# Attention scores masked by VectorE in PSUM, with ScalarE copying the products with V and turned v

## The chip, the cores and the metric

The kernel runs on one core of a Trainium2 chip. A core has four engines that matter here, each with its own list of instructions, in order: TensorE (matrix products and the turning of tiles, which write PSUM), VectorE, ScalarE and GpSimd; SyncE issues the loads. Semaphores order them. The metric is the device time of one execution in microseconds (us), the median of several runs.

## The reference, cut to what matters

Two blocks follow each other. The first one is two layers of attention on 1024 tokens behind 16 meta tokens (L = 1040), in float32. Each layer has 4 "diff" heads, each with two score maps whose softmaxes are subtracted, and 8 "fox" heads with a forget term. Scores are masked: in diff heads by chunks of 64 tokens, in fox heads causally.

```python
# diff: chunk_ids is 0 for the meta tokens, then one number for each 64 tokens
s = einsum('bhmqd,bhmkd->bhmqk', qb, k) * scale
s = where(chunk_ids[None, :] <= cq[:, None], s, -inf)
p = softmax(s)
a = p[:, :, 0] - lam * p[:, :, 1]
o = einsum('bhqk,bhkd->bhqd', a, v)
# fox
s = einsum('bhqd,bhkd->bhqk', qb, k) * scale + cq[..., None] - cum_logf
s = where(positions[None, :] <= pq[:, None], s, -inf)
o = einsum('bhqk,bhkd->bhqd', softmax(s), v)
```

The second block (retention, a Fourier mix, a convolving feed-forward part) isn't touched by the change.

## The kernel before, in words

Products are made from split numbers: each float32 operand is kept as a high part rounded for TensorE (WH, AH, QH, KH) and a low rest (WL, AL, QL, KL), and three products (high by high, high by low, low by high) stand for one. ScalarE rounds the weights (L1596), VectorE makes the rests (L2173).

A layer's attention has 8 groups g of 128 rows: g below 4 is one diff head with its two maps m, g of 4 and more ("fox" in the code) two fox heads. Its work is a list of steps:

- a unit (`step_unit`, L1048) is one eighth of a projection's chunk of 344, 352 or 512 columns: three products with all 128 rows of the array. Projections of later groups fill the time between the other steps;
- scores (`step_scores`, L1094): for a block j of 128 query rows (j = 0 to 7; 8 is the 16 meta rows, in layer 0 alone) the scores of both maps. Their width W is 16 + 128 (j + 1), or 16 for j = 8. Map m uses rows 64m to 64m + 63 of the array, so products of the two maps stand in pairs. Each span of PSUM up to a bank's edge (512 columns) has three products, in fox a fourth with the forget term (C2, selr). Then come the mask products (`masks`, L1118): eyer, an identity of 64 rows, by maskr, which adds -1e30 at the hidden places. Diff has one on the last 64 columns, none at j = 8; fox one on the last 128 (16 at j = 8) and one on the last 64, cut at the banks' edges. Scores have one region of PSUM for each map (`region`, L351), so a block's scores wait for the exp of the block before;
- max (`step_max`, L2350): VectorE reduces each map's row maximum from PSUM; exp (`step_exp`, L1732): ScalarE makes exp(s - max) into P and its row sum; norm (`step_norm`, L2360): VectorE scales P;
- tr (L1152): TensorE turns tiles of P into one of the banks 5, 6 and 7 (`turn_bank`, L1041); pt: ScalarE (L1755) or VectorE (L2392 to L2395) copies them out;
- turn_v (L1085) turns v into such a bank, v_out (`step_v_out`, L2337) copies it to V, four tiles of 128 x 128 at a time and one of 16 x 128;
- av (L1170) makes the products of turned P with V in such a bank, av_out (`step_av_out`, L2397) copies them to OTt, which is gated (L2429), stored by GpSimd and loaded again at the layer's end. A group's first av_out waits for the store of the group before.

The order of the steps is written by a planner, `attention_order` (L761), with a class `Clocks` (L399): it keeps a time for each engine, gives each step a cost (`cost`, L439, for TensorE; `side_of`, L575, for the others), and places the step that can begin next, by rank. Each engine then takes its own steps from that one list. `PRIORITY` and `ACT_STEPS` (L402 to L405) say how side steps rank and which of them are ScalarE's. The wait of a copy stands in front of it on whichever engine it is.

At the start, ScalarE's `step_set_up` (L1674) copies the constants eyer, maskr and selr from where SyncE's loads put them, inside V (L158, L3115), and the first v_out waits for that. Of the lines in the trace, L977 is every matrix product and L986 every turning.

Of the kernel before, what the change touches and what calls it, by code (L numbers as in the profile page):

```python
# [7 lines left out]
F32R = mybir.dt.float32r  # L8
ALU = mybir.AluOpType
# [94 lines left out]
def build(nc, A, S, O):  # L104

    ctx = ExitStack()
    with ctx:
# [50 lines left out]
        SELF, MASKF = Vf[:, 0:1024], Vf[:, 1024:1664]  # L158
# [240 lines left out]
        class Clocks:  # L399
# [5 lines left out]
            ACT_STEPS = ("leave", "exp", "rope_end", "split", "fin1", "root", "reload")  # L405
# [33 lines left out]
            def cost(self, st):  # L439
# [135 lines left out]
            def side_of(self, st):  # L575
# [462 lines left out]
        def tensor_attention(e, l):  # L1038
# [55 lines left out]
            def step_scores(g, j):  # L1094
                fox = g >= 4
                if l == 0 and g == 0:
                    e.wait_ge(*const_split.at(0))
# [20 lines left out]
                def masks(m, a, b):  # L1118

                    r = slice(64 * m, 64 * m + 64)  # L1120
                    d0 = 0 if j == 8 else W - 128
                    if fox:
                        c0, c1 = max(a, d0), b
                        if c0 < c1:
                            yield eyer[r, 0, :], maskr[r, 1, c0 - d0:c1 - d0], c0, c1
                    if j != 8:
                        c0, c1 = max(a, W - 64), b
                        if c0 < c1:
                            yield eyer[r, 1 if fox else 0, :], maskr[r, 2 if fox else 0, c0 - W + 64:c1 - W + 64], c0, c1
# [452 lines left out]
        def scalar(e):  # L1582
# [79 lines left out]
            def attention(l):  # L1662
# [61 lines left out]
                def step_rope_end(g, kind, ci):  # L1724
# [5 lines left out]
                    e.activation((QH if kind == "q" else KH)[:, g % 2, c:c + n], TMP[:, c:c + n], ACT.Copy).then_inc(*qk_hi.mark(key))  # L1730

# [54 lines left out]
                do = {"split": step_split, "leave": step_leave, "fill": step_fill, "stats": step_stats, "set_up": step_set_up, "forget": step_forget, "rope_end": step_rope_end, "exp": step_exp, "pt": step_pt,  # L1786
# [379 lines left out]
        def vector(e):  # L2166
# [74 lines left out]
            def attention(l):  # L2241
# [95 lines left out]
                def step_v_out(g, quad):  # L2337
                    vs = g % 2
                    b = banks.place.get(("vt", l, g, quad), 0)
                    e.wait_ge(*vt_mm.at((l, g, quad)))  # L2340
                    if quad == 0 and g == 0 and l == 0:
                        e.wait_ge(*const_split.at(0))
                    if quad == 0 and g >= 2:
                        e.wait_ge(*av_mm.at((l, g - 2, len(BLOCKS[l]) - 1)))
                    if quad < 2:
                        e.tensor_copy(V[:, vs, 4 * quad:4 * quad + 4, :], bank(b).rearrange("p (a b) -> p a b", a=4)).then_inc(*v_turned.mark((l, g, quad)))
                    else:
                        e.tensor_copy(V[0:NM, vs, 8, :], bank(b)[0:NM, 0:128]).then_inc(*v_turned.mark((l, g, quad)))
# [48 lines left out]
                def step_av_out(g, bi):  # L2397
                    blk = BLOCKS[l][bi]
                    meta = blk == (8,)
                    nq = NM if meta else 256  # L2400
                    q0 = 0 if meta else NM + 128 * blk[0]
                    b = banks.place.get(("av", l, g, bi), 0)
                    e.wait_ge(*av_mm.at((l, g, bi)))
                    if bi == 0:
                        if g:
                            e.wait_ge(*o_stored.at((l, g - 1)))
                        elif l:
                            e.wait_ge(*fill_tr.at((1, 4, 7)))
                    e.tensor_copy(OTt[:, q0:q0 + nq], bank(b)[:, 0:nq]).then_inc(*av_out.mark((l, g, bi)))

# [26 lines left out]
                def step_stats(p):  # L2437
# [3 lines left out]
                      "forget": step_forget, "rope_sin": step_rope_sin, "rope_add": step_rope_add, "rope_lo": step_rope_lo, "v_out": step_v_out,  # L2441
                      "max": step_max, "norm": step_norm, "pt": step_pt, "av_out": step_av_out, "fin_ms": step_fin_ms, "fin3": step_fin3,
# [657 lines left out]
        def sync(e):  # L3100
# [14 lines left out]
            e.dma_start(MASKF, A["k_mask"]).then_inc(*const_in[1].landed(0))  # L3115
# [54 lines left out]
def host_constants():  # L3170
# [4 lines left out]
    r = np.arange(64)  # L3175
    m = np.zeros((2, 64, 5, 128), f)
    for a in range(2):
        m[:, r, a, 64 * a + r] = 1.0
    m[:, :, 2, 0:64] = NEG
    m[:, :, 3] = np.where(q[None, :] <= r[:, None], 0.0, NEG)  # L3180
    m[:, :, 4, 0:64] = np.where(r[None, :] <= r[:, None], 0.0, NEG)
    c["k_mask"] = m.reshape(128, 640)
# [100 lines left out]
```

## Time and profile before

| what | us |
|---|---|
| median of 3 runs | 2811.51 |
| the runs | 2808.3, 2811.51, 7464.21 |
| the profiled execution | 2806.45 |
| its span, first to last instruction | 2804.6 |
| the attention of layer 0, about | 80 to 743 of the span |
| the attention of layer 1, about | 890 to 1510 of the span |

All durations below come from the profiled execution. Busy time of TensorE counts overlapping products once, and the row of one product lasts longer than the distance to the next one's start, since products are pipelined; the distance between starts tells what one costs. The granted clock is 2.4 GHz nearly throughout (a mean of 0.99 of it).

### The profile page before, as it was taken

The page shows a single profiled execution, that of the slowest core. Times are in us where ns is not written, and L with a number is a line of the kernel's source. Part 1 is how long each engine was busy: PE and PEld are TensorE (multiplying, and loading weights), DVE is VectorE, ACT ScalarE, POOL GpSimd, SP SyncE. Part 2 cuts the span into 40 slices and gives each one's busy share as a digit, 9 for nine tenths or more (in the row PEclk, how much of TensorE's full clock was granted, in tenths as well). Part 3 has the DMA queues.
Part 4 walks back from the last instruction along what each step waited for, and adds up shares of the span by engine and source line. Part 5 has one row for each costly group of instructions (what it writes and reads, how often), then busy time and mean ns, then how long its engine had stood idle before and what let it go on. Part 6 is the DMA issues. An engine that isn't in the chain of part 4 may idle for free.

```text
span 2804.6 us, 42406 instructions
## 1 busy us (share of the span) xinstructions
PE 2731.3 (97%) x17076; PEld 2347.9 (84%) x17076; DVE 1533.5 (55%) x2769; ACT 1035.8 (37%) x1967; POOL 258.6 (9%) x392
## 2 busy tenths in 40 slices
PE   6999999999999999999999999999999999999999
PEld 6788888888899888877787988888998888888887
DVE  5766654555546666655445485564365444455335
ACT  5434333333334444433334562224362222223232
POOL 1211100000002122000002060000030000000000
PEclk9999999999999999999999999999999999999999
DMA  4111211111312212122114132212331111111113
GB/s 151 62 62 58 74 59 59 59 57 62 130 63 67 70 63 80 59 65 71 63 38 143 59 109 65 60 38 97 106 113 46 53 45 53 46 50 56 53 60 128
DMA packets 149185, 200.11 MB, mean 71 GB/s; under 512 B 8806, under 2 KB 117030, under 8 KB 148990
## 3 DMA queue, kind: packets, MB, share of 16 engines
q1 hardware_dynamic: 128064, 134.20, 15.3%
q0 software_dynamic: 20928, 63.20, 6.3%
q8 instruction: 137, 2.24, 0.3%
q14 instruction: 56, 0.46, 0.1%
HBM read 162.66 MB, written 32.58 MB: 70 GB/s over the span
## 4 chain that ended last, share of the span: by engine, by line
PE 85%; DVE 6%; ACT 3%; issue 3%; DMA 2%; POOL 1%; DVEq 0%; SPq 0%; ACTq 0%; POOLq 0%
PE PS L977 80%; PE PS L986 5%; DMA T<-TMP 2%; DVE ST L2358 1%; DVE AL L2216 1%; POOL TMP L2979 0%; DVE WL L2173 0%; ACT top L1742 0%; DVE TMP L2328 0%; POOL T L2976 0%; DMA s_os<-OTt 0%; DVE T L2321 0%; DVE top L2371 0%; ACT WH L1596 0%; ACT TMP L1718 0%
## 5 line engine op out<-in xcount | busy, mean ns | idle before, releaser
L977 PE MATMUL PS<-AH,WH 128*128 128x512 f32 (+3 forms) x2528 | 941.7, 372 | 18.7 <-DVE AL L2216 9.3
L977 PE MATMUL PS<-AL,WH 128*128 128x512 f32 (+3 forms) x2528 | 895.1, 354 | 0.0
L977 PE MATMUL PS<-AH,WL 128*128 128x512 f32 (+3 forms) x2528 | 894.4, 354 | 0.0
L977 PEld LDWEIGHTS PS<-AH,WH 128*128 128x128 f32 x2528 | 477.1, 189 | 91.8 <-issue 18.3
L977 PEld LDWEIGHTS PS<-AH,WL 128*128 128x128 f32 x2528 | 476.7, 189 | 48.0
L977 PEld LDWEIGHTS PS<-AL,WH 128*128 128x128 f32 x2528 | 478.1, 189 | 45.0 <-issue 1.0
L977 PE MATMUL PS<-WH,AH 128*128 128x256 f32 (+1 forms) x1016 | 326.4, 321 | 4.0 <-DVE WL L2173 3.1
L2173 DVE TENSOR_TENSOR WL<-W,WH 128x1024 fp32r<-128x1024 f32 x184 | 225.6, 1229 | 185.0 <-ACT WH L1596 185.0
L977 PE MATMUL PS<-WL,AH 128*128 128x256 f32 (+1 forms) x1016 | 325.6, 320 | 0.0
L977 PE MATMUL PS<-WH,AL 128*128 128x256 f32 (+1 forms) x1016 | 325.5, 320 | 0.0
L2358 DVE TENSOR_REDUCE ST<-PS 128x1 f32<-128x784 f32 (+8 forms) x272 | 187.6, 731 | 126.9 <-PE PS L977 126.8
L1596 ACT ACTIVATE WH<-W 128x1024 fp32r<-128x1024 f32 x184 | 193.4, 1053 | 160.7 <-PE PS L977 140.4
L1742 ACT ACTIVATE top<-PS,ST 128x784 f32<-128x784 f32 (+8 forms) x272 | 195.1, 723 | 142.3 <-DVE ST L2358 115.7
L977 PEld LDWEIGHTS PS<-WH,AH 128*128 128x128 f32 x1016 | 193.7, 191 | 20.6 <-DVE WL L2173 3.9
L977 PEld LDWEIGHTS PS<-WL,AH 128*128 128x128 f32 x1016 | 193.7, 191 | 13.9
L977 PEld LDWEIGHTS PS<-WH,AL 128*128 128x128 f32 x1016 | 193.7, 191 | 13.6
L986 PE MATMUL PS<-ident,top 128*128 128x128 f32 (+2 forms) x1132 | 172.6, 276 | 12.7 <-DVE AL L2216 3.0
L977 PE MATMUL PS<-top,V 128*64 128x256 f32 (+6 forms) x1176 | 182.5, 371 | 1.4 <-DVE top L2395 0.8
L2092 ACT ACTIVATE R<-PS,R 128x512 f32<-128x512 f32 x88 | 68.4, 779 | 295.4 <-PE PS L977 295.4
L977 PEld LDWEIGHTS PS<-top,V 128*64 128x64 f32 (+3 forms) x1176 | 119.2, 154 | 64.8 <-issue 36.9
L2893 DVE SCALAR_TENSOR_TENSOR R<-PS,R 128x504 f32<-128x504 f32 x88 | 65.3, 742 | 185.7 <-ACT R L2092 185.7
L986 PEld LDWEIGHTS PS<-ident,top 128*128 128x128 f32 (+2 forms) x1132 | 125.5, 132 | 45.2 <-ACT top L1755 6.9
(341 smaller groups left out, 3347.8 us busy)
## 6 DMA issues: line engine op xcount, KB each, us to landing
W<-in_k_w_in SPq DMA_DIRECT2D x66, 512.0 KB, 3.9
W<-in_w_ada SPq DMA_DIRECT2D x48, 512.0 KB, 4.9
W<-in_w_up SPq DMA_DIRECT2D x44, 512.0 KB, 3.8
W<-in_w_in SPq DMA_DIRECT2D x28, 512.0 KB, 3.7
W<-in_w_out SPq DMA_DIRECT2D x24, 512.0 KB, 3.4
W<-in_w_down SPq DMA_DIRECT2D x22, 512.0 KB, 3.6
R<-s_xs POOLq DMA_DIRECT2D x16, 512.0 KB, 6.9
s_adap<-AST POOLq DMA_DIRECT2D x48, 128.0 KB, 4.4
```

The source lines that it names most:

```text
L977: return e.matmul(out, lhsT, rhs, start=start, stop=stop, skip_group_check=True)
L986: return e.transpose(out, in_, ident[0:k, 0:k])
L1596: e.activation(high(v), W32[:, s, :], ACT.Copy).then_inc(*w_hi.mark(v))
L1742: e.activation(P[0:rows, P_SLOT[u], 0:W], PSf[0:rows, o:o + W], ACT.Exp, bias=st[:, 0:1], accum_out=st[:, 1:2]).then_inc(*exped.mark(u))
L2092: e.activation(dst[:, c:c + n], bank(b), ACT.Identity, scale=CW[:, 1, jj:jj + 1], bias=CW[:, 3, jj:jj + 1]).then_inc(*conv_a.mark((j, ab, ...
L2173: e.tensor_tensor(low(v), W32[:, slot32(v), :], f(high(v)), ALU.subtract).then_inc(*w_lo.mark(v))
L2216: e.scalar_tensor_tensor(lo, bank(b)[:, o:o + n], COLS[:, 8 * l + k:8 * l + k + 1], f(hi), ALU.mult, ALU.subtract).then_inc(*fill_lo.mark( ...
L2358: e.tensor_reduce(ST[0:rows, ST_SLOT[u], 0:1], PSf[0:rows, o:o + W], AX.X, ALU.max, negate=True).then_inc(*row_max.mark(u))
L2893: e.scalar_tensor_tensor(d3[:, :, 1:64], o3[:, :, 0:63], CW[:, 0, jj:jj + 1], d3[:, :, 1:64], ALU.mult, ALU.add).then_inc(*conv_v.mark((j, ...
```

## The change

TensorE's mask products go, and with them eyer and maskr. A tile MK of its own takes the mask constants as they are loaded: a causal 128 x 128 one for both maps side by side, and a 64 x 64 one of -1e30 for the upper half of a diff block's rows. VectorE's `step_max` adds the mask to both maps in PSUM with one instruction (its pattern spans both regions), marks a semaphore, waits for it, and then makes the two reductions. Diff blocks add on 64 rows and 2 x 64 columns, fox blocks on 128 rows and 2 x 128 columns (16 rows and 2 x 16 at j = 8), diff j = 8 nothing. av_out and v_out are ScalarE's, with the same waits. The planner's costs follow.

```diff
-            eyer = own("eyer", [128, 2, 128], F32R)
-            maskr = own("maskr", [128, 3, 128], F32R)
+            MK = own("MK", [128, 640])[:, :]
...
+        CAUSAL, BLOCKED = MK[:, 0:256].rearrange("p (m n) -> p m n", m=2), MK[0:64, 256:384].rearrange("p (m n) -> p m n", m=2)
...
-            ACT_STEPS = ("leave", "exp", "rope_end", "split", "fin1", "root", "reload")
+            ACT_STEPS = ("leave", "av_out", "v_out", "exp", "rope_end", "split", "fin1", "root", "reload")
...
-                    return sum((4 if g >= 4 else 3) * max(110, 8 + 0.44 * (b - a)) for a, b in cut) + (250 if j != 8 else 0) + (90 if g >= 4 else 0)
+                    return sum((4 if g >= 4 else 3) * max(110, 8 + 0.44 * (b - a)) for a, b in cut)
...
-                    return max(at[("scores",) + st[1:]], at[("normed",) + self.stats[i - 4]] if i >= 4 else 0.0), 300 + 2.08 * width(st[2])
+                    return (max(at[("scores",) + st[1:]], at[("normed",) + self.stats[i - 4]] if i >= 4 else 0.0),
+                            300 + 2.08 * width(st[2]) + (450 if st[1] >= 4 else 320 if st[2] != 8 else 0))
...
-                if l == 0 and g == 0:
+                if l == 0 and g == 4:
                     e.wait_ge(*const_split.at(0))
...
-                        row += [(q, k, c0, c1, False) for q, k, c0, c1 in masks(m, a, b)]
...
                 def step_set_up():
                     e.wait_ge(*const_in[1].at("all"))
-                    e.activation(eyer[:, :, :].rearrange("p a b -> p (a b)"), MASKF[:, 0:256], ACT.Copy)
-                    e.activation(maskr[:, :, :].rearrange("p a b -> p (a b)"), MASKF[:, 256:640], ACT.Copy)
...
+                    e.activation(OTt[:, q0:q0 + nq], bank(b)[:, 0:nq], ACT.Copy).then_inc(*av_out.mark((l, g, bi)))
...
+                        e.activation(V[:, vs, 4 * quad:4 * quad + 4, :], bank(b).rearrange("p (a b) -> p a b", a=4), ACT.Copy).then_inc(*v_turned.mark((l, g, quad)))
...
                 def step_max(g, j):
                     rows, W = (NM if j == 8 else 128), width(j)
+                    fox = g >= 4
+                    for m in range(2):
+                        e.wait_ge(*score_mm[m].at((l, g, j)))
+                    if fox or j != 8:
+                        if l == 0 and g == 0:
+                            e.wait_ge(*const_in[1].at("all"))
+                        n = min(W, 128) if fox else 64
+                        mask = CAUSAL[0:rows, :, 0:n] if fox else BLOCKED
+                        a, apart = region(j, 0) + W - n, region(j, 1) - region(j, 0)
+                        late = PSf[0:rows if fox else 64, a:a + 2 * apart].rearrange("p (m n) -> p m n", m=2)[:, :, 0:n]
+                        e.tensor_tensor(late, late, mask, ALU.add).then_inc(*row_max.mark((l, g, j, "masked")))
+                        e.wait_ge(*row_max.at((l, g, j, "masked")))
                     for m in range(2):
...
-                        e.wait_ge(*score_mm[m].at((l, g, j)))
...
-                    e.tensor_copy(OTt[:, q0:q0 + nq], bank(b)[:, 0:nq]).then_inc(*av_out.mark((l, g, bi)))
...
-            e.dma_start(MASKF, A["k_mask"]).then_inc(*const_in[1].landed(0))
+            e.dma_start(MK, A["k_mask"]).then_inc(*const_in[1].landed(0))
```

## Rows read from the trace of the kernel before

**Rows 1.** The page: busy time, share of the span and instructions of each engine.

```profile
PE 2731.3 (97%) x17076; PEld 2347.9 (84%) x17076; DVE 1533.5 (55%) x2769; ACT 1035.8 (37%) x1967; POOL 258.6 (9%) x392
```

**Rows 2.** Busy time by stretch: us, PE, PEld, DVE, ACT, POOL, clock, DMA share, GB/s.

```profile
80.00:743.00 663.00, 643.07 (x4683) 554.05 (x4681) 392.68 (x867) 253.99 (x543) 64.11 (x101) 0.99 0.19 64
890.00:1510.00 620.00, 606.30 (x4167) 497.49 (x4164) 371.80 (x777) 247.00 (x494) 62.07 (x94) 1.00 0.20 66
...
1490.00:1510.00 20.00, 16.47 (x135) 11.37 (x135) 17.91 (x45) 12.77 (x27) 1.58 (x3) 0.98 0.25 79
```

**Rows 3.** Waits of TensorE in 80 to 743 us: us, times, longest.

```profile
PE PS L977 <- DVE OTt L2409: 3.1, 4, 2.5
...
PE PS L977 <- ACT top L1742: 1.3, 3, 0.5
```

**Rows 4.** Waits of TensorE in 890 to 1510 us.

```profile
PE PS L977 <- ACT top L1742: 5.5, 10, 1.3
```

**Rows 5.** The tile maskr: its products, min/median/max ns, first and last start, forms.

```profile
L977 PE MATMUL PS<-maskr,eyer x416: 182/234/267, 88.8 to 1503.3; 64*128 64x64 f32 x77, 64*128 64x128 f32 x40, 64*128 64x16 f32 x13, 64*128 64x48 f32 x8
```

**Rows 6.** Timeline of TensorE around a fox step, 912 columns: start, us, engine, instruction.

```profile
503.99 0.31 PE L977 MATMUL PS<-AH,WL 128*128 128x344 f32 x1
504.23 0.50 PE L977 MATMUL PS<-KH,QH 64*128 64x512 f32 x2
...
505.81 0.34 PE L977 MATMUL PS<-C,selr 64*128 64x400 f32 x2
505.99 0.30 PE L977 MATMUL PS<-maskr,eyer 64*128 64x128 f32 x4
506.23 0.42 PE L977 MATMUL PS<-AH,WH 128*128 128x344 f32 x1
```

**Rows 7.** The same around the end of a diff step, 528 columns.

```profile
125.93 0.28 PE L977 MATMUL PS<-KH,QL 64*128 64x256 f32 x2
126.05 0.19 PE L977 MATMUL PS<-maskr,eyer 64*128 64x64 f32 x2
126.17 0.43 PE L977 MATMUL PS<-AH,WH 128*128 128x344 f32 x1
```

**Rows 8.** The same around the end of a diff step of 16 columns, without mask.

```profile
159.02 0.26 PE L977 MATMUL PS<-KL,QH 64*128 64x16 f32 x2
...
159.13 0.26 PE L977 MATMUL PS<-KH,QL 64*128 64x16 f32 x2
...
159.32 0.43 PE L977 MATMUL PS<-AH,WH 128*128 128x344 f32 x1
```

**Rows 9.** Groups of VectorE by shape: count, busy us, mean ns, idle before.

```profile
L2409 DVE COPY OTt<-PS 128x256 f32<-128x256 f32 x64 | 27.1, 423 | 83.7 <-PE PS L977 77.4 <-DMA s_os<-OTt 6.4
...
L2346 DVE COPY V<-PS 128x512 f32<-128x512 f32 x32 | 20.7, 684 | 7.7 <-PE PS L986 7.7
...
L2308 DVE SCALAR_TENSOR_TENSOR GT<-GT,PS 128x344 f32<-128x344 f32 x16 | 8.1, 509 | 15.1 <-ACT GT L1711 15.0
```

**Rows 10.** Groups of ScalarE by shape.

```profile
L1755 ACT ACTIVATE top<-PS 128x512 f32<-128x512 f32 x101 | 59.4, 597 | 82.1 <-PE PS L986 81.4
...
L1755 ACT ACTIVATE top<-PS 16x256 f32<-16x256 f32 x61 | 22.6, 372 | 115.5 <-PE PS L986 115.5
```

**Rows 11.** Timeline of ScalarE's set-up copies.

```profile
50.34 0.41 ACT L1676 ACTIVATE eyer<-V 128x256 fp32r<-128x256 f32 x1
...
50.65 0.51 ACT L1677 ACTIVATE maskr<-V 128x384 fp32r<-128x384 f32 x1
```

**Rows 12.** Timeline of the first block of layer 0, with idle time and its releaser.

```profile
92.22 1.13 ACT L1742 ACTIVATE top<-PS,ST 128x1040 f32<-128x1040 f32 x1 [2.29 <-DVE ST L2358]
...
92.84 0.38 PE L986 MATMUL PS<-ident,TMP 128*16 128x128 f32 x1 [2.44 <-DVE V L2346]
```

**Rows 13.** Timeline: two VectorE instructions, the second of which reads the first's result.

```profile
94.91 0.75 DVE L2371 TENSOR_SCALAR top<-top,ST 128x1040 f32<-128x1040 f32 x1
...
95.78 1.30 DVE L2374 SCALAR_TENSOR_TENSOR top<-top,ST 128x1040 f32<-128x1040 f32 x1
```

More of the change, by code:

```diff
@@ L157, in build @@
         Vf = V.rearrange("p s t n -> p (s t n)")
-        SELF, MASKF = Vf[:, 0:1024], Vf[:, 1024:1664]
+        SELF = Vf[:, 0:1024]
+        CAUSAL, BLOCKED = MK[:, 0:256].rearrange("p (m n) -> p m n", m=2), MK[0:64, 256:384].rearrange("p (m n) -> p m n", m=2)
         LAMT, LAMP = GT[:, 0:512].rearrange("p (l a n) -> p l a n", l=2, a=4), GT[:, 512:640].rearrange("p (a n) -> p a n", a=2)
@@ L1116, in terms @@
                         yield selr[r, 2 * (g - 4) + m, :], C2[r, a:b]
[L1118 to L1129, printed above, removed]
                 cuts = [[(x - region(j, m), y - region(j, m)) for x, y in pieces(region(j, m), region(j, m) + W)] for m in range(2)]
@@ L1730, in step_rope_end, with step_av_out, step_v_out @@
                     e.activation((QH if kind == "q" else KH)[:, g % 2, c:c + n], TMP[:, c:c + n], ACT.Copy).then_inc(*qk_hi.mark(key))
+                def step_av_out(g, bi):
+                    blk = BLOCKS[l][bi]
+                    meta = blk == (8,)
+                    nq = NM if meta else 256
+                    q0 = 0 if meta else NM + 128 * blk[0]
+                    b = banks.place.get(("av", l, g, bi), 0)
+                    e.wait_ge(*av_mm.at((l, g, bi)))
+                    if bi == 0:
+                        if g:
+                            e.wait_ge(*o_stored.at((l, g - 1)))
+                        elif l:
+                            e.wait_ge(*fill_tr.at((1, 4, 7)))
+                    e.activation(OTt[:, q0:q0 + nq], bank(b)[:, 0:nq], ACT.Copy).then_inc(*av_out.mark((l, g, bi)))
+                def step_v_out(g, quad):
+                    vs = g % 2
+                    b = banks.place.get(("vt", l, g, quad), 0)
+                    e.wait_ge(*vt_mm.at((l, g, quad)))
+                    if quad == 0 and g == 0 and l == 0:
+                        e.wait_ge(*const_split.at(0))
+                    if quad == 0 and g >= 2:
+                        e.wait_ge(*av_mm.at((l, g - 2, len(BLOCKS[l]) - 1)))
+                    if quad < 2:
+                        e.activation(V[:, vs, 4 * quad:4 * quad + 4, :], bank(b).rearrange("p (a b) -> p a b", a=4), ACT.Copy).then_inc(*v_turned.mark((l, g, quad)))
+                    else:
+                        e.activation(V[0:NM, vs, 8, :], bank(b)[0:NM, 0:128], ACT.Copy).then_inc(*v_turned.mark((l, g, quad)))
                 def step_exp(g, j):
@@ L1784, in step_stats @@
                     norm_stats(l, p)
-                do = {"split": step_split, "leave": step_leave, "fill": step_fill, "stats": step_stats, "set_up": step_set_up, "forget": step_forget, "rope_end": step_rope_end, "exp": step_exp, "pt": step_pt,
+                do = {"split": step_split, "leave": step_leave, "fill": step_fill, "stats": step_stats, "set_up": step_set_up, "forget": step_forget, "rope_end": step_rope_end, "exp": step_exp, "av_out": step_av_out, "v_out": step_v_out, "pt": step_pt,
                       "fin1": step_fin1, "root": step_root, "reload": step_reload}
@@ L2335, in step_rope_lo @@
                     e.tensor_tensor(lo[:, g % 2, c:c + n], TMP[:, c:c + n], f(hi[:, g % 2, c:c + n]), ALU.subtract).then_inc(*qk_lo.mark(key))
[L2337 to L2348, printed above, removed]
                 def step_max(g, j):
                     rows, W = (NM if j == 8 else 128), width(j)
+                    fox = g >= 4
[10 more added lines that the diff above has]
+                        e.wait_ge(*row_max.at((l, g, j, "masked")))
                     for m in range(2):
@@ L2395, in step_pt @@
                         e.tensor_copy(PT[:, pt, part[1], 128:256], bank(b)[:, 384:512]).then_inc(*pt_dve.mark(key))
[L2397 to L2408, printed above, removed]
-                    e.tensor_copy(OTt[:, q0:q0 + nq], bank(b)[:, 0:nq]).then_inc(*av_out.mark((l, g, bi)))
                 def step_fin_ms(g, ci):
@@ L2440, in attention @@
                 do = {"split_lo": step_split_lo, "leave_lo": step_leave_lo, "fill": step_fill, "stats": step_stats, "set_up": step_set_up, "ada_out": step_ada_out,
-                      "forget": step_forget, "rope_sin": step_rope_sin, "rope_add": step_rope_add, "rope_lo": step_rope_lo, "v_out": step_v_out,
-                      "max": step_max, "norm": step_norm, "pt": step_pt, "av_out": step_av_out, "fin_ms": step_fin_ms, "fin3": step_fin3,
+                      "forget": step_forget, "rope_sin": step_rope_sin, "rope_add": step_rope_add, "rope_lo": step_rope_lo,
+                      "max": step_max, "norm": step_norm, "pt": step_pt, "fin_ms": step_fin_ms, "fin3": step_fin3,
                       "gate": step_gate, "reload_lo": step_reload_lo}
@@ L3174, in host_constants @@
     q = np.arange(128)
[L3175 to L3182, printed above, removed]
+    m = np.zeros((128, 640), f)
+    m[:, 0:256] = np.tile(np.where(q[None, :] <= q[:, None], 0.0, NEG), 2)
+    m[0:64, 256:384] = NEG
+    c["k_mask"] = m
     s = np.zeros((128, 8, 128), f)
```

## The prediction, made before the change was run

> **What bounds the kernel now.** The page comes first: TensorE is busy 97% of the span, VectorE 55%, ScalarE 37% [rows 1]. The change touches only the two attention stretches, so the table by stretch is next: in 80 to 743 us TensorE is busy for 643.1 of 663 us, in 890 to 1510 for 606.3 of 620 [rows 2]. It therefore stands still for 19.9 + 13.7 = 33.6 us there. VectorE has 392.7 + 371.8 = 764.5 us of work in these 1283 us (60%), ScalarE 254.0 + 247.0 = 501 us (39%). Then the waits of TensorE by releaser: for the exp that frees the score banks 1.3 us in 3 waits and 5.5 us in 10, for VectorE's copy of a product with V 3.1 us [rows 3, 4]. Attention is bound by TensorE's own work, and time taken out of that work is gained as long as what replaces it stays beside it. Other parts of the kernel are left alone.
>
> **Part 1, the mask products leave TensorE.** There are 416 [rows 5]. By the code: a diff step with j of 0 to 6 has two (one pair, the halves m = 1 and 0 run side by side on 64 rows each), j = 7 has three; a fox step has four, j = 7 six, j = 8 two. Over both layers 68 x 2 + 136 x 2 + 8 = 416 (block 8 is in layer 0 alone).
> What one costs is read between starts, since durations overlap. In a fox step the four begin at 505.99 and the next projection unit at 506.23: 0.24 us [rows 6]. In a diff step 126.05 to 126.17: 0.12 us [rows 7]. If all of that went, the sum would be 56 x 0.12 + 56 x 0.25 + the sixteen j = 7 steps at about 0.25 and 0.6 + four j = 8 steps at 0.2: 6.7 + 14 + 2 + 4.8 + 0.9 = 28 us, and some 33 us if the mixed ends of the steps (masks ahead of a transposition or a product with V, not shown) are up to a sixth dearer. This is the upper bound.
> But part of this interval isn't the mask's. In the other direction, from a unit of 344 columns (503.99) to the first score pair (504.23), 0.24 us pass [rows 6]; 344 columns at 2.4 GHz are 0.143 us, so changing between 128-row and 64-row products costs about 0.1 us. The diff pair of 64 columns is 0.027 us of streaming; 0.12 less 0.027 leaves the same 0.09. That gap stays when the mask goes: it then stands behind the last score pair. So a diff mask gives back only its streaming, 0.03 us. The next limit is the weight load: pairs of 16 columns follow each other every 0.11 us [rows 8]. Where the last score pair is short (144 columns, j = 0 and 4), the mask pair waited for its load, and 0.05 us more goes. In a fox step the second pair (64 columns) is loaded while the first streams, so it costs a whole load: 0.11 + 0.03 = 0.14 us. Step by step: diff 40 x 0.03 + 16 x 0.08 = 2.5; diff j = 7, 8 x 0.2 = 1.6 (two short loads in one half); fox 40 x 0.14 + 16 x 0.19 = 8.6; fox j = 7, 8 x 0.37 = 3.0 (three to four loads in one half); j = 8, 4 x 0.11 = 0.4. Sum 16 us. This is the lower bound, and the one I take, because the two gaps of rows 6 and 7 agree on it.
> The Trainium skill says the same of the gap, in "TensorEngine Tiling (Array Packing)", section "Key Properties": changing the tiling mode drains TensorE. By that rule the gap is owed at every change, mask or no mask, and the sum is 16 us; without it it would be 28 to 33. The trace agrees as far as it goes (0.24 us behind a unit, 0.12 behind a mask pair), but has no wide score step without a mask to show it.
>
> **Part 2, VectorE's masks.** 64 fox steps get an addition on 128 x 256 elements of PSUM, 64 diff steps one of 64 x 128, four one of 16 x 32: 132 in all. No row shows an addition that writes PSUM. The nearest reads it: 128x344 in 509 ns, and 128x512 copied in 684 ns, so 151 ns and 1.04 ns an element [rows 9]. That gives 0.42 us and 0.28 us. Below, the 0.12 us of hand-over could be hidden; above, I allow 0.1 us for the write into PSUM. The first reduction reads the result and waits for it; between two such dependent instructions 95.66 to 95.78 pass, 0.12 us [rows 13]. Added: 64 x 0.42 + 64 x 0.28 + 0.7 + 132 x 0.12 = 61 us.
> The wait for the scores isn't new: the reductions waited for the same products. What is behind it in VectorE's queue (its copies of turned P, the low halves of the weights) gets each time 0.4 to 0.54 us later, and so does the exp, which frees the single pair of score regions.
>
> **Part 3, the copies go to ScalarE.** VectorE loses 64 copies at 423 ns and 32 at 684 ns [rows 9], with 16 of 128 columns (0.28 us by the same rule) and 8 of 16: 27 + 21 + 4.5 + 1.3 = 54 us. So VectorE ends at +7 us, 60% busy as before. ScalarE takes them at 372 ns for 256 columns and 597 ns for 512 [rows 10]: 24 + 19 + 4 + 1.4 = 48 us, 549 of 1283 us, 43% busy. Neither becomes the bound by its work. But a copy on ScalarE now stands behind two exps (1.13 us each for the widest block [rows 12]), and the copy frees one of TensorE's three turning banks. TensorE waited 3.1 us for these copies in the first stretch [rows 3]; I let it lose 2 us more. VectorE's 6.4 us of waiting for the store of the last group's output [rows 9] goes to ScalarE with the copy; the exps behind it are then held, 0 to 6 us, taken as 0, since the list of steps is planned with the store's due time.
> One place gains. At 92.84 TensorE has waited 2.44 us for VectorE's copy of turned v, which stood behind two reductions, while ScalarE was idle for 2.29 us before its exp at 92.22 [rows 12]. There the copy gets done at once: 0 to 2.4 us, I take 2.
>
> **Part 4, set-up and loads.** ScalarE's two copies into eyer and maskr go: 0.41 + 0.51 us [rows 11]. They stand ahead of the rounding of the weights for which TensorE waits at about 58 us, so 0.9 us is gained, 0 at worst. SP issues the same two loads; the mask's lands in a tile of its own.
>
> **Part 5, the order.** The planner gets new costs (TensorE's 250 and 90 ns go, 450 and 320 come to VectorE, the copies to ScalarE), so the interleaving changes throughout. It can't win more than what TensorE now stands still, 33.6 us, and a poorer fit could cost as much as a third of that again. The latency has a plainer price: TensorE waited 13 times for the exp that frees the score banks; each grows by about 0.4 us, together +5 us. The end of layer 1 is the tight place: in 1490 to 1510 VectorE is busy 17.9 of 20 us [rows 2]; four steps' masks (2 us) enter and three copies (1.3 us) leave, +0.7 us, part of these 5.
>
> **Sum.** -16 - 0.9 - 2 + 5 + 2 = -12 us. The profiled execution took 2806.45 us (span 2804.6): 2794.5 us. The fast two of the runs shown are 2808.3 and 2811.5, 2 to 5 us above it, so I say 2795 us. A measurement of this kernel can tell about 2% (56 us) from no change.
>
> **Rivals.**
> - The whole interval of the masks goes (28 to 33 us), the array's change being hidden under the wide score pair. For: the next weights could load meanwhile. Against: rows 6. 2806.5 - 30 - 2.9 + 7 = 2780 us, 2777 with 33.
> - Given back: ScalarE's queue order and the changed plan cost what TensorE gains, some 12 us more than counted. For: TensorE's waits in attention are only 33.6 us because the plan fits so well. 2806 us.
> - Slower: the turn-round of the score banks. The banks are held from the first score product to the second exp; the mask lengthens this by 0.54 less 0.14 us in fox, 0.40 less 0.03 in diff, about 0.4 us a step. Once the steps at which TensorE runs out of other work pass 19 / 0.4 = 48 of 136, the gain is gone; the trace has 13. At 90 steps it is +36 - 19 = +17 us: 2824 us; at all 136 (no product's time gained, the chain alone deciding) +54, 2860 us. Against it: the same 13 waits, 6.8 us in 1283, so the chain has slack at the other 123 steps.
>
> **How the numbers follow.** Forecast 0.50, whole interval 0.17, given back 0.18, turn-round 0.15. The forecast's own range is 2786 to 2803. The range goes from the whole interval with its larger sum (2777, less 2) to halfway between given back and turn-round: 2775 to 2813. Over 2% faster (below 2750) needs more than all mask intervals and both gains, 36 us: 0.02. Over 2% slower needs every step in the chain and more: 0.02. Within 2%: 0.96.
>
> **What would show it.** TensorE without any maskr rows and 416 instructions fewer, busy time and start-to-start of the stretches down by some 16 us; a fox step of 8 pairs (912 columns) taking 1.86 us where it was 2.00 [rows 6], and a gap of about 0.1 us behind its last pair beyond streaming. If it takes 1.75, the first rival holds. An addition row of about 420 and 285 ns, and the reduction 0.12 us behind it. Waits of TensorE for the exp up from 6.8 us to about 12; if they are above 25 us, the turn-round holds. ScalarE 48 us busier. I am wrong if attention gets longer, or if TensorE's waits move by more than 15 us in either direction.

## The result, and the profile after

The changed kernel takes 2817.14 us (median of 12 runs, 2811.24 to 2819.25) against 2810.8 us for the kernel before on the same chip: a ratio of 1.0023, 95% interval 1.0015 to 1.0031. That is within the 2% called "same", but it is a small loss where a gain of 12 us was forecast, and it lies above the range. The profiled execution has a span of 2816.8 us (2804.6 before).

The page's busy line of the kernel after:

```profile
PE 2727.8 (97%) x16660; PEld 2335.5 (83%) x16660; DVE 1536.0 (55%) x2778; ACT 1078.1 (38%) x2088; POOL 261.3 (9%) x392
```

TensorE has exactly 416 instructions fewer [rows 1], ScalarE 42 us more work, VectorE as much as before. By stretch (columns as in [rows 2]):

```profile
80.00:743.00 663.00, 638.17 (x4464) 546.20 (x4464) 398.29 (x872) 274.32 (x606) 66.47 (x101) 0.98 0.20 66
890.00:1510.00 620.00, 598.53 (x3904) 485.36 (x3900) 360.58 (x756) 260.55 (x533) 60.67 (x92) 0.98 0.20 63
```

TensorE stands still for 24.8 + 21.5 = 46.3 us where it was 33.6, and the clock is 0.98 in both stretches where it was 0.99 and 1.00. The new instructions, by shape (the first two to be held against the forecast of 420 and 280 ns, the last two against 372 and 597):

```profile
L2361 DVE TENSOR_TENSOR PS<-PS,MK 128x256 f32<-128x256 f32 x64 | 27.6, 431 | 93.3 <-PE PS L978 93.0
L2361 DVE TENSOR_TENSOR PS<-PS,MK 64x128 f32<-64x128 f32 x64 | 18.4, 288 | 49.2 <-PE PS L978 48.9
...
L1729 ACT ACTIVATE OTt<-PS 128x256 f32<-128x256 f32 x64 | 24.6, 384 | 133.9 <-PE PS L978 129.8 <-DMA s_os<-OTt 4.1
L1740 ACT ACTIVATE V<-PS 128x512 f32<-128x512 f32 x32 | 17.3, 594 | 18.7 <-PE PS L987 18.7
```

The fox step of 912 columns, which went from 504.23 to 506.23 [rows 6], in TensorE's timeline after:

```profile
508.72 0.50 PE L978 MATMUL PS<-KH,QH 64*128 64x512 f32 x2
...
510.29 0.36 PE L978 MATMUL PS<-C,selr 64*128 64x400 f32 x2
510.58 0.43 PE L978 MATMUL PS<-AH,WH 128*128 128x344 f32 x1
```

510.58 - 508.72 = 1.86 us, as forecast, not 1.75. The last pair streams 400 columns (0.17 us at 2.4 GHz) and the next unit starts 0.29 us behind it: 0.12 us are owed for the change of products, mask or not. The first rival ends here.

Now the waits. TensorE's in 80 to 743 us, then in 890 to 1510 us:

```profile
PE PS L978 <- ACT top L1754: 8.0, 6, 2.8
PE PS L978 <- DVE top L2402: 3.7, 2, 2.0
PE PS L987 <- ACT TMP L1703: 3.2, 1, 3.2
```

```profile
PE PS L978 <- ACT top L1754: 9.9, 7, 3.4
PE PS L978 <- DVE FIN L2411: 4.8, 3, 2.9
```

Those for the exp (L1754, L1742 before [rows 3, 4]) are again 13, but 17.9 us in place of 6.8, with single ones of 2.8 and 3.4 us where the longest was 1.3. An addition of 0.43 us can't make such a wait. The longest, with all engines, in order of time (idle time and releaser in brackets):

```profile
1088.95 1.23 DVE L2425 SCALAR_TENSOR_TENSOR OTt<-OTt,GT 128x1024 f32<-128x1024 f32 x1
...
1090.09 0.22 DVE L2377 RECIPROCAL ST<-ST 128x1 f32<-128x1 f32 x2
...
1090.58 0.60 POOL L2979 DMA_DIRECT2D s_os<-OTt  x1 [7.26 <-DVE OTt L2425]
...
1091.13 0.90 DVE L2384 SCALAR_TENSOR_TENSOR top<-top,ST 128x656 f32<-128x656 f32 x1
1091.24 0.28 PE L978 MATMUL PS<-KH,QL 64*128 64x256 f32 x2
...
1091.95 0.42 DVE L2265 COPY AST<-PS 128x256 f32<-128x256 f32 x1
1092.29 0.28 DVE L2361 TENSOR_TENSOR PS<-PS,MK 64x128 f32<-64x128 f32 x1
1092.60 1.32 DVE L2368 TENSOR_REDUCE ST<-PS 128x1 f32<-128x528 f32 x2
1093.34 0.70 ACT L1754 ACTIVATE top<-PS,ST 128x528 f32<-128x528 f32 x1 [2.79 <-DVE ST L2368]
...
1094.62 0.20 ACT L1754 ACTIVATION_READ_ACCUMULATOR top<-PS,ST 128x1 f32 x1
1094.91 0.70 PE L978 MATMUL PS<-KH,QH 64*128 64x400 f32 x2 [3.39 <-ACT top L1754]
```

The scores of 528 columns end at 1091.5, and TensorE's next step is the scores of 400 columns, for which there is no room until both exps have read the scores. VectorE is behind: the gate of the group that ends here and the last block's normalisation are ahead of the addition, and only then come the two reductions and the exps. TensorE takes its list in order, so what stands behind the scores waits with them. The new order has four such places (202.35, 286.33, 1010.31 and 1094.91 us), score step directly behind score step; the old order has none. What follows a long wait is seen behind the second of them:

```profile
286.33 0.70 PE L978 MATMUL PS<-KH,QH 64*128 64x400 f32 x2 [2.74 <-ACT top L1754]
...
288.37 0.49 PE L978 MATMUL PS<-AH,WL 128*128 128x344 f32 x1
288.66 0.49 PE L978 MATMUL PS<-AH,WH 128*128 128x344 f32 x1
...
292.62 0.32 PE L978 MATMUL PS<-AH,WL 128*128 128x344 f32 x1
292.78 0.32 PE L978 MATMUL PS<-AH,WH 128*128 128x344 f32 x1
```

Up to about 292.5 the same products of 344 columns start every 0.29 us, afterwards every 0.16: 344 columns take 0.287 us at 1.2 GHz and 0.143 at 2.4. The trace's record of the granted clock has 6.8 us at the lower level here, from 285.71 to 292.54, so it fell 0.6 us before the wait ended. (The Trainium skill, "TensorE: Matmul & The Clock Gate", Part 1, says that an idle TensorE is put to half rate; the trace agrees.)

**An account of the attention.** Three numbers of a trace say where each kernel's time goes, from 85 us to the start of its last score step: the gaps between TensorE's products; the time in which products ran at 1.2 GHz by the record of the granted clock (half of which is lost; the part of a slow stretch that falls into a gap is in the gaps already and is left out); and the rest, which is work at 2.4 GHz. All in us. The first column is the median of the kernel's runs; the others are of one profiled execution each, which lies up to 6 us from that median (both_copies_order's took 2781.3). The kernels of the next section are in the table too:

| kernel | median | last score step | gaps | products at 1.2 GHz | last - gaps - half |
|---|---|---|---|---|---|
| before | 2810.8 | 1502.7 | 33.6 | 9.3 | 1464.4 |
| after | 2817.1 | 1514.1 | 49.4 | 44.2 | 1442.7 |
| masks_old_order | 2808.9 | 1504.9 | 44.8 | 19.6 | 1450.3 |
| both_old_order | 2822.2 | 1515.5 | 51.3 | 31.0 | 1448.7 |
| copies_old_order | 2825.9 | 1523.3 | 41.9 | 34.1 | 1464.3 |
| new_order_alone | 2855.5 | 1554.2 | 67.5 | 53.8 | 1459.8 |
| no_masks_old_order | 2800.6 | 1498.6 | 36.9 | 25.2 | 1449.1 |
| copies_own_order | 2788.3 | 1487.2 | 23.8 | 13.0 | 1456.9 |
| both_copies_order | 2786.7 | 1480.6 | 30.8 | 13.7 | 1443.0 |
| fox_masks_copies_order | 2784.0 | 1481.4 | 29.1 | 13.4 | 1445.6 |
| two_pairs | 2797.8 | 1499.3 | 40.5 | 31.7 | 1442.9 |
| one_pair | 2806.7 | 1505.9 | 44.2 | 34.1 | 1444.7 |
| no_pairs | 2814.7 | 1509.6 | 49.1 | 32.9 | 1444.1 |

After against before: 21.8 us less of work, 15.7 us more of gaps, 17.5 us more lost to the clock, +11.4 at the last score step. The work saved was real; more than all of it went to gaps and the clock. Not all of the 21.8 us is the mask products: the four pairs of kernels that share an order and differ in the masks differ by 14.0 to 17.2 us, and the rest goes with the order (new_order_alone, with every product of before, has 4.6 us less work than before).

### The profile page after: what moved, and what is told of

Its sections match the earlier page's. It is cut to its first block, busy times and chain, and to the rows that moved or that the text cites. A ratio compares the mean times of both kernels' runs of the same rounds, so it can differ in the third digit from the quotient of the medians.

```text
span 2816.8 us, 41701 instructions
## 1 busy us (share of the span) xinstructions
PE 2727.8 (97%) x16660; PEld 2335.5 (83%) x16660; DVE 1536.0 (55%) x2778; ACT 1078.1 (38%) x2088; POOL 261.3 (9%) x392
## 4 chain that ended last, share of the span: by engine, by line
PE 87%; DVE 4%; ACT 3%; issue 3%; DMA 2%; POOL 0%; SPq 0%; ACTq 0%; DVEq 0%; POOLq 0%
PE PS L978 82%; PE PS L987 5%; DMA T<-TMP 1%; DVE AL L2228 1%; ACT top L1754 0%; DVE WL L2185 0%; DVE ST L2368 0%; DMA s_os<-OTt 0%; ACT TMP L1595 0%; ACT TMP L1703 0%; ACT R L1888 0%; ACT L1780 0%; ACT R L1820 0%; ACT WH L1583 0%; POOL T L2972 0%
## 5 line engine op out<-in xcount | busy, mean ns | idle before, releaser
L1754 ACT ACTIVATE top<-PS,ST 128x784 f32<-128x784 f32 (+8 forms) x272 | 194.9, 722 | 121.9 <-DVE ST L2368 101.6
```

The costliest lines, as they stand in the source:

```text
L1754: e.activation(P[0:rows, P_SLOT[u], 0:W], PSf[0:rows, o:o + W], ACT.Exp, bias=st[:, 0:1], accum_out=st[:, 1:2]).then_inc(*exped.mark(u))
```

## The experiments

Two words recur. **Old order** means that the planner lists the steps as for the kernel before, whatever the engines then do. **Own order** means that it is given the costs of what is kept. Theories under test at first: the masks' latency ate the gain; the copies on ScalarE ate it; or the new order did. The letters in an expectation are explained in it. All ratios are to the kernel before on the same chip, with the 95% interval. The groups of kernels ran on different chips, on which the kernel before took 2808.5 to 2810.8 us, so a difference of two medians can be off by some 2 us; the difference of the two ratios is given beside it where that matters.

**1. The order, and each part in the old order.** Four kernels. both_old_order is the changed kernel with the planner's lines as before:

```
-            ACT_STEPS = ("leave", "av_out", "v_out", "exp", ...)
+            ACT_STEPS = ("leave", "exp", ...)
-                    return sum(...)
+                    return sum(...) + (250 if j != 8 else 0) + (90 if g >= 4 else 0)
-                            300 + 2.08 * width(st[2]) + (450 if st[1] >= 4 else 320 if st[2] != 8 else 0))
+                    ... 300 + 2.08 * width(st[2])
```

> Edit: the changed kernel with the planner's costs and its list of ScalarE steps as they were before, so every engine goes by the list of steps of the kernel before. Theory A (the new order is what lost the time: TensorE gives back 14 us of mask products as it should, and the list planned with the new costs puts score steps where they wait): 2795 to 2802 us, 9 to 16 us under before, TensorE's waits in attention no more than 8 us above before's, no new stretch at 1.2 GHz. Theory B (the mask in the chain from scores to exp costs this directly, wherever it is put): 2812 us or more, and TensorE's waits for the exp up by 10 us or more. Theory C (the copies behind the exps in ScalarE's queue): also above 2808 us, with waits of TensorE for the copies at their ScalarE lines.

masks_old_order also takes step_av_out and step_v_out back to VectorE (tensor_copy), copies_old_order instead takes the mask products back and the additions out, and new_order_alone is the kernel before with the three planner edits of the change alone.

> Edit: the masks on VectorE alone; the copies stay on VectorE, and the order is that of before. Theory A: 2797 to 2804 us, VectorE 61 us busier. Theory B: above 2812 us, as with the copies moved. Theory C: 2797 us or less, clearly under the run with the copies on ScalarE.

> Edit: the kernel before with the two kinds of copies on ScalarE alone; masks stay products, order of before. Theory A: 2805 to 2812 us, within 4 us of before. Theory B: the same. Theory C: 2815 us or more, with TensorE waiting for the copies more than 10 us.

> Edit: the kernel before in every instruction, but planned with the changed costs and with the copies counted as ScalarE's, so only the order of the steps is new. Theory A: 2822 to 2835 us, the 16 us of waits and some 27 us more at 1.2 GHz being all there (mask products stay, so 14 us more than the changed kernel at most). Theories B and C: 2806 to 2815 us, like before.

Measured: both_old_order 2822.2 us, 1.0047 [1.0034, 1.0059]; masks_old_order 2808.9 us, 0.9995 [0.9987, 1.0004]; copies_old_order 2825.9 us, 1.0063 [1.005, 1.0076]; new_order_alone 2855.5 us, 1.0164 [1.015, 1.0178]. So the masks are neutral, the copies lose 17 us in an order that was not made for them, and an order made for other engines costs 46 us with no work changed. Theory A's ranges missed all four: the old order did not bring the changed kernel back (2822 us for 2795 to 2802), and new_order_alone, slower as it said, came out 20 us above its range. masks_old_order fits none of the three theories. Theory C was right for copies_old_order. What that kernel loses is, by the account, 8.3 us of gaps and 12.4 us of clock. Among TensorE's waits in 80 to 743 us are:

```profile
PE PS L977 <- DVE GT L2335: 6.3, 3, 3.0
PE PS L977 <- ACT V L1755: 4.0, 4, 3.4
PE PS L986 <- ACT OTt L1744: 3.0, 2, 1.5
```

The last two are copies. That they wait their turn in a list of ScalarE's that was not made for them is my reading; the run of part 3 that changes the list alone bears it out.

**2. What the additions cost.** The changed kernel without them, in the old order with the copies on VectorE; the masks are left out, so this kernel computes attention unmasked:

```
-                        e.tensor_tensor(late, late, mask, ALU.add).then_inc(...)
-                        e.wait_ge(*row_max.at((l, g, j, "masked")))
```

> Edit: as masks_old_order, with VectorE's mask addition and its wait left out, so the scores aren't masked at all; order of before. What this leaves is TensorE's saving alone. If the saving is real and VectorE's mask in the chain gives it back (theory D: latency): 2793 to 2799 us, 10 to 16 us under masks_old_order. If time freed on TensorE is lost anyway, because the other engines' chains hold the places where it stalls (theory E: no cover): 2803 to 2809 us, with TensorE's idle time up by what was saved.

Measured 2800.6 us, 0.996 [0.9947, 0.9972]. The additions, 132 of them, cost 2808.9 - 2800.6 = 8.3 us (10 by the ratios) where the prediction had 5. The time lies between the ranges of D and E. Taking the products away brings 10 us net, of 15.3 us less work by the account (before 1464.4, this kernel 1449.1).

**3. Each part in its own order.** masks_own_order has the new mask costs with copies and their planner entry on VectorE; copies_own_order is copies_old_order with one line more:

```
-            ACT_STEPS = ("leave", "exp", ...)
+            ACT_STEPS = ("leave", "av_out", "v_out", "exp", ...)
```

> Edit: the masks on VectorE with the planner's new costs for them, the copies on VectorE and planned there. Theory D (latency, which an order that knows of it can hide): 2797 to 2804 us, under masks_old_order. Theory E or a plan that is merely another one: 2806 to 2820 us.

> Edit: the copies on ScalarE and planned there, the masks as products with their old costs. If the 17 us of copies_old_order come from an order that didn't know of the move (theory F): 2806 to 2812 us. If they come from the place itself, behind the exps (theory C): 2818 us or more.

Measured: masks_own_order 2809.6 us, 1.0006 [0.9995, 1.0016]; copies_own_order 2788.3 us, 0.992 [0.9906, 0.9934]. That one line is worth 38 us, and the copies alone beat the kernel before by 22 us, more than either theory allowed: both ranges for copies_own_order lie 17 us and more above it. masks_own_order fell into the range of theory E. Its busy line and its table by stretch:

```profile
PE 2722.6 (98%) x17076; PEld 2347.2 (84%) x17076; DVE 1489.2 (53%) x2652; ACT 1079.7 (39%) x2084; POOL 255.4 (9%) x392
```

```profile
80.00:735.00 655.00, 641.67 (x4704) 557.61 (x4704) 373.56 (x806) 279.05 (x607) 63.71 (x101) 0.99 0.20 67
890.00:1500.00 610.00, 602.03 (x4142) 494.70 (x4143) 346.89 (x719) 260.04 (x540) 61.50 (x99) 1.00 0.21 67
```

TensorE stands still for 13.3 + 8.0 us of these 1265. In the same two windows of the kernel before:

```profile
80.00:735.00 655.00, 636.05 (x4626) 547.23 (x4625) 387.71 (x863) 248.70 (x537) 60.56 (x95) 0.99 0.18 60
890.00:1500.00 610.00, 599.83 (x4114) 493.40 (x4111) 362.61 (x753) 240.62 (x480) 61.28 (x93) 1.00 0.20 64
```

it was 18.9 + 10.2 us. By the account the gaps fall by 9.9 us, the clock takes 1.9 more, and 7.5 us are less work at 2.4 GHz for the same instructions. That goes with the order (copies_old_order, with the same instructions in the order of before, has the work of before), but I can't attribute it further.

**4. One kind of copy alone.** The 48 copies of turned v on ScalarE, those of the products with V on VectorE, old order (step_v_out alone moves):

> Edit: of the two kinds of copies only that of turned v is on ScalarE; masks as products, order of before. The copies of v are 16 us of VectorE's 54 but stand at few places. If the loss follows the number of copies (72 of products, 48 of v): 2813 to 2817 us. If it comes from v alone, whose bank and whose V tile TensorE waits for: 2820 us or more; from the products' copies alone: 2807 to 2811 us.

Measured 2814.6 us, 1.0015 [1.0006, 1.0025]: 4 us, a quarter of what both kinds lose in the old order, in the range for a loss that follows the number of copies.

**5. The changed kernel in the copies' order.** The decisive one: the same instructions as the changed kernel, only the planner's two mask costs are the old ones.

```
-                    return sum(...)
+                    return sum(...) + (250 if j != 8 else 0) + (90 if g >= 4 else 0)
-                            300 + 2.08 * width(st[2]) + (450 if st[1] >= 4 else 320 if st[2] != 8 else 0))
+                    ... 300 + 2.08 * width(st[2])
```

> Edit: the changed kernel, planned with the copies as ScalarE's but with the masks' costs of before, so that its order is that of copies_own_order (2788 us), into which the masks on VectorE are put. Theory H (the masks themselves cost what they save, as masks_old_order showed, and the 29 us between copies_own_order and the changed kernel come from the order that the masks' new costs make): 2784 to 2795 us, no two score steps next to each other on TensorE. Theory D (the mask's latency costs it where the copies wait in ScalarE's queue): 2803 us or more.

copies_nudged asks whether the copies' order is a lucky one: copies_own_order with 240 in place of the planner's 250, which was meant to reorder steps.

> Edit: copies_own_order with one cost of the planner changed by 10 ns (a score step's masks 240 instead of 250), nothing else; it gives another order. If an order's luck is a matter of a few us: 2784 to 2794 us. If small changes of cost throw the time about: further from 2788 than 8 us, and then no difference of that size between two orders can be read as an effect of what was planned.

Measured: both_copies_order 2786.7 us, 0.9922 [0.9908, 0.9935]; copies_nudged 2787.2 us, 0.9918 [0.9905, 0.9932]. So the change as a whole does gain 22 us, with the planner's two mask costs left alone, and theory H holds. These two costs, which describe its masks, lose 30 us (28 by the ratios). The nudge proves little: in the traces TensorE's products of copies_own_order and copies_nudged stand in the same order but for fewer than 80 of 9757, where before and copies_own_order differ in some 3350. It shows that almost the same order takes the same time, not that the copies' order isn't a lucky one; that rival is not tested. At the place of the 3.39 us wait TensorE's timeline of both_copies_order reads

```profile
1073.89 0.32 PE L977 MATMUL PS<-AL,WH 128*128 128x344 f32 x1
1074.05 0.32 PE L977 MATMUL PS<-AH,WL 128*128 128x344 f32 x1
1074.30 0.45 PE L977 MATMUL PS<-KH,QH 64*128 64x400 f32 x2
1074.59 0.34 PE L977 MATMUL PS<-KL,QH 64*128 64x400 f32 x2
1074.76 0.35 PE L977 MATMUL PS<-KH,QL 64*128 64x400 f32 x2
1075.04 0.43 PE L977 MATMUL PS<-AH,WH 128*128 128x344 f32 x1
```

with projection units ahead of the scores of 400 columns, and no wait.

**6. The fastest mixture.** Fox masks by VectorE, diff masks by products as before (at the start ScalarE copies the smaller eyer and maskr, and the causal mask into MK), copies on ScalarE, the planner's mask costs old:

```
-                    if fox or j != 8:
+                    if g >= 4:
...
+                    if not fox and j != 8:
+                        c0, c1 = max(a, W - 64), b
+                        if c0 < c1:
+                            yield eyer[r, :], maskr[r, c0 - W + 64:c1 - W + 64], c0, c1
```

> Edit: copies_own_order with VectorE's masks in the fox groups alone (diff keeps its one pair of mask products, which cost 0.03 us a step; 12 of the 14 us that the masks save on TensorE are in fox). Order as copies_own_order. Theory H with the waits of masks_old_order in the diff groups: 2776 to 2785 us, the fastest so far. Theory D: 2790 us or more.

Measured 2784.0 us (2783.6 to 2784.3), 0.991 [0.9897, 0.9924]: the lowest of all, ahead of both kernels, though its interval overlaps those of both_copies_order and copies_own_order. By the account the fox masks give TensorE 11.4 us in 68 steps (0.17 each) and the diff masks 2.6 us in 64 (0.04 each), for an addition each.

**7. Are the four long waits the masks'?** The changed kernel in its own order without the additions (the masks are left out again):

> Edit: the changed kernel with VectorE's mask addition and its wait left out, so the scores aren't masked; order of the changed kernel. Theory H (the order has four places where one score step follows another and TensorE waits 2.7 to 3.4 us for the exp between them): 2802 to 2812 us, those four waits still over 2 us each. Theory D: 2795 us or less, the waits gone.

Measured 2809.2 us, 0.9997 [0.9989, 1.0006]. 8.0 us go (7 by the ratios), as in the old order; the four waits stay, 2.40, 2.40, 2.40 and 3.40 us. They belong to the order: new_order_alone, whose masks are products, has them at the same four steps too, with 2.38, 2.38, 2.39 and 3.02 us.

**8. Are they the cause of the 30 us?** Three kernels with the changed kernel's instructions. two_pairs keeps the old cost of the maximum, one_pair the old cost of the scores, and no_pairs has both new ones but may not list scores right behind scores:

```
-                    if queue:
+                    if queue and not (queue is scores and clocks.last == "scores"):
```

> The changed kernel whole, instruction for instruction the same work (masks added by VectorE, copies on ScalarE); only the planner's cost of the step max is the old one (no 450 or 320 ns for a mask), while TensorE's cost of the scores is the new one. By the planner's list two score steps stand right behind each other in groups 1 and 2 of layer 0, and nowhere in layer 1. Theory A (the time goes with these adjacent score steps: a wait of 2.4 to 3.4 us in each, and 1.2 GHz behind it): the changed kernel had four of them and 2817 us, both_copies_order none and 2787 us, so some 7.5 us each: 2802 us here (2795 to 2808), the stretches of 1.2 GHz behind the pairs in layer 0 and none of that kind in layer 1. Theory B (the order as a whole does not fit, the pairs are one sign among others): no proportion; 2810 to 2820 us is as likely as 2790. Theory C (the new cost of the step max is the one that spoils the order): within 4 us of 2787.

> The changed kernel whole; only the planner's cost of the scores on TensorE is the old one (250 and 90 ns for mask products kept), while the cost of the step max has the new 450 and 320 ns. By the planner's list one pair of adjacent score steps is left, in group 2 of layer 1. Theory A: one pair, 2787 + 7.5 = 2795 us (2790 to 2799), with one wait of over 2.4 us and 1.2 GHz behind it near 1090 us. Theory B: no proportion, up to 2810 to 2817. Theory C (the cost of the step max spoils it): 2810 us or more.

> The changed kernel with its new costs, both of them; only the planner may not place a score step right behind a score step, so that something else of TensorE comes between. Theory A: no pair is left and 2787 to 2797 us, with no wait of over 2 us between score steps and at most 10 us at 1.2 GHz within the attention. Theory B: the waits move to other places and the time stays at 2808 to 2820 us.

Measured: two_pairs 2797.8 us, 0.996 [0.9947, 0.9972]; one_pair 2806.7 us, 0.9991 [0.9981, 1.0001]; no_pairs 2814.7 us, 1.0021 [1.0012, 1.0029]. Only two_pairs came out as the theory of the pairs said; one_pair missed its range by 8 us and no_pairs by 18, and no_pairs came out as theory B said. One pair costs more than two, and none costs nearly as much as four: the theory of the pairs has fallen. So has the one that blames the cost of the maximum alone: TensorE's new cost is worth +11 us by itself, VectorE's +20, both together +30. What no_pairs did with the place is seen in TensorE's timeline:

```profile
1085.83 0.28 PE L980 MATMUL PS<-KH,QL 64*128 64x256 f32 x2
1091.66 0.66 PE L980 MATMUL PS<-AH,WH 128*128 128x344 f32 x1 [5.55 <-ACT OTt L1731]
...
1092.40 0.49 PE L980 MATMUL PS<-AH,WL 128*128 128x344 f32 x1
```

and in ScalarE's:

```profile
1087.92 0.70 ACT L1756 ACTIVATE top<-PS,ST 128x528 f32<-128x528 f32 x1 [2.78 <-DVE ST L2370]
...
1091.23 0.38 ACT L1731 ACTIVATE OTt<-PS 128x256 f32<-128x256 f32 x1 [1.83 <-DMA s_os<-OTt]
```

The scores of 528 columns are followed by a unit, and that unit waits longer still, for the copy of a product with V, which waits for the store of the group before. At the other three places the unit waits 2.97, 2.97 and 2.98 us for such a copy, where the scores had waited 2.74 or 2.75. As I read it, every bank is held at this point of the list by something that the end of the group is late for: scores by exps behind the gate, turning banks by a copy behind the store. Which step stands next then decides only what is waited for. No run moves these steps alone, so this is argued, not shown. What is shown is that only gaps and clock make the difference: the five kernels with the changed kernel's instructions and the copies in the planner's list (after, both_copies_order and these three) have 1442.7 to 1444.7 us of work, and the last score steps of after and both_copies_order, with 1442.7 and 1443.0, are 33.5 us apart.

## Why the prediction was wrong

- **Part 1, right.** Forecast 16 us off TensorE. By the account 14.2 us between before and masks_old_order, 15.6 between copies_old_order and both_old_order, 14.0 between copies_own_order and both_copies_order and 17.2 between new_order_alone and after, each pair in one order. The wide fox step took 1.86 us, as said; the change of products is owed with or without a mask. The rule of the Trainium skill that was weighed there ("TensorEngine Tiling (Array Packing)", "Key Properties") is borne out by the 0.12 us behind the last wide pair.
- **Part 2, right in prices.** 431 and 288 ns for 420 and 280. The reduction starts 0.31 us behind the start of the diff addition (1092.29, 1092.60), which leaves 0.03 us of hand-over where I counted 0.12: 0.31 us of latency a step for my 0.40. Over the whole page VectorE ended at +2.5 us for +7, ScalarE at +42 for +48.
- **The latency, mis-sized.** "+5 us" from 13 waits that grow by 0.4: the additions measured 8.3 and 8.0 us. And one order's gaps went up by 11.2 us with the masks (before to masks_old_order), the clock's loss by 5.2: waits in new places and the clock were missing from the sum.
- **Part 3, wrong.** I had the copies at +2 us less 2 at the start. The start was right (the wait of 2.44 us [rows 12] is 0.25 now). But the copies are worth -22 us in an order made for them and +17 in the old one. Why they gain is argued, not shown, and so is that an order made for them, and not a lucky one, is what it takes: I read VectorE's and ScalarE's load as harmless, since neither bounds, and so gave no value to freeing VectorE's list: it is the list in which the reductions stand, on which exp and banks hang.
- **Part 4, mis-sized.** TensorE's wait at about 58 us for the rounding of the weights fell from 1.54 to 1.17 us (1.17 in masks_old_order and 1.16 in both_copies_order, which have no set-up copies either, 1.54 in copies_own_order, which keeps them): 0.4 us for my 0.9.
- **Part 5 is the step that failed.** "It can't win more than what TensorE now stands still, 33.6 us, and a poorer fit could cost as much as a third of that again": I wrote down both ends and then put the order into the sum at nothing but the latency. It moved by 30 us (the two mask costs, given the copies; 28 by the ratios), by 35 us (the copies' entry: both_old_order to both_copies_order), and by 46 us with the old work (new_order_alone), each above my third, 11 us. With the copies on VectorE the same two mask costs moved it by 0.7 us (masks_old_order to masks_own_order; 3 by the ratios, whose intervals overlap): costs interact, which a sum over parts can't show.
- **The clock was not in the sum at all**, though the rows of before give it by stretch [rows 2]. It carries 17.5 of the 33 us that were given back.
- **Rivals.** "Given back" had the right kind (the plan), 2806 us, and too small a size. The turn-round of the banks as I priced it, by additions, is not what happened, since without them the waits stay; but the place it named, banks that nothing frees in time, is where the time went as I read the traces. "Waits for the exp about 12 us" came to 17.9, below the 25 set for that rival.
- **The range and the signs.** Halfway between 2806 and 2824 us is 2815, not the 2813 of the range; the measured 2817 lies above both. Of the two signs of being wrong, attention did get longer (+11.4 us at the last score step), while TensorE's waits moved by 12.7 us, short of 15. And a difference from no change can be told far below 2% (56 us): the interval of the ratio here is 0.16% wide.
- **Not settled:** why the planner's simulation, given truer costs, ends in a poorer list; which steps of a group's end have to move; whether the copies' order is a lucky one; and the 5 to 8 us of work that differ between orders.

## What to carry to other kernels

Where an order of steps is planned from costs, a change of engine is two changes: time the new work in the old order, and the new order with the old work, before adding anything up. Here the first was worth +13 us, the second +46, and both together, with the planner's two mask costs left alone, -22. Here truer costs did not make a better plan; keep an order that is measured to be good. And where the record shows products at 1.2 GHz behind a wait of TensorE, count half of their time with the wait: from before to after that half grew by more than the gaps did.

## What the runs showed of the hardware that was not expected

In the kernel after, a single wait of 2.74 us (286.33) came with 6.8 us at 1.2 GHz, of which 6.2 us ran products, so that it cost 3.1 us more than the wait itself. Products at 1.2 GHz came to 9.3 us in the attention of the kernel before and 44.2 in the one after, and that difference cost more (17.5 us) than the longer gaps themselves (15.7 us). Not every such wait had a slow stretch behind it: waits of 2.18 us (855.0, before) and 2.08 us (1166.5, after) had none. And ScalarE copied the same tiles out of PSUM faster than VectorE had: 384 against 423 ns for 128x256 and 594 against 684 ns for 128x512 [rows 9].
